# Down weights of each expert loaded from ACT's DMA queue, up weights still from SP's

## What is computed

```python
def expert_block(args):
    xb, e = args
    gate, up = jnp.split(xb @ w_up[e], 2, axis=-1)
    return (jax.nn.silu(gate) * up) @ w_down[e]
```

## Time and profile before

| | |
|---|---|
| median of three executions | 1182.05 us |
| profiled execution | 1187.32 us |
| its span, first to last instruction | 1185.6 us |
| TensorE clock granted, mean of the span | 0.936 |
| busy share PE / DVE / ACT / POOL | 86 / 81 / 53 / 43 % |
| SP's and ACT's queue, data moved | 270.65 MB / 0.20 MB |
| up loads, issue to landing, median | 128 x 1 MB, 7.0 us |
| down loads, issue to landing, median | 64 x 1 MB, 7.4 us |

### The profile page before, as it was taken

How to read it: one execution, slowest core, us unless ns; L and a number is a source line. 1 busy time by engine, 2 the same in 40 slices (tenths; PEclk the granted TensorE clock), 3 DMA queues, 4 the chain that set the end, 5 groups by cost and what they waited for, 6 DMA issues and landing times.

```text
span 1185.6 us, 15716 instructions
## 1 busy us (share of the span) xinstructions
PE 1018.2 (86%) x5224; PEld 843.9 (71%) x5224; DVE 954.8 (81%) x1003; ACT 627.0 (53%) x580; POOL 508.8 (43%) x314
## 2 busy tenths in 40 slices
PE   0888899999989985853999999999999999999960
PEld 0667679778867964853788887787877778888750
DVE  6686973995697398775788988889889899988868
ACT  1343452445345344052666776766767677776740
POOL 1343544545454454411534444664346545536110
PEclk9888999999998997855999999999999999999995
DMA  9233524432442345053889999999999999999973
GB/s 359 74 82 96 143 59 130 131 96 81 142 142 71 124 125 177 1 180 118 320 299 338 363 360 353 359 368 350 344 358 358 364 357 373 372 365 365 336 254 146
DMA packets 102892, 279.61 MB, mean 236 GB/s; under 512 B 10035, under 2 KB 59339, under 8 KB 85455
## 3 DMA queue, kind: packets, MB, share of 16 engines
q1 hardware_dynamic: 96874, 270.65, 63.9%
q0 software_dynamic: 4640, 8.41, 2.0%
q10 hardware_dynamic: 1350, 0.20, 0.1%
HBM read 275.03 MB, written 12.58 MB: 243 GB/s over the span
## 4 chain that ended last, share of the span: by engine, by line
DVE 22%; DMA 20%; PE 14%; issue 7%; ACT 6%; SPq 0%; DVEq 0%; ACTq 0%; POOLq 0%; POOL 0%
DMA moe<-in_moe_w_up 10%; DMA moe<-in_moe_w_down 9%; DVE moe_r L1105 8%; ACT moe_r L739 5%; PE ps L1546 3%; PE ps L1548 3%; PE ps L1550 2%; PE ps L1479 1%; DVE ssd L891 1%; PE ps L1504 1%; PE ps L1481 1%; PE ps L1480 1%; DVE moe L1202 1%; DVE moe_r L1208 1%; DVE moe_r L1196 1%
## 5 line engine op out<-in xcount | busy, mean ns | idle before, releaser
L1105 DVE TENSOR_TENSOR moe_r<-moe,moe_r 128x2048 fp32r<-128x2048 f32 x192 | 444.2, 2327 | 68.1 <-ACT moe_r L739 66.9
L739 ACT ACTIVATE moe_r<-moe 128x2048 fp32r<-128x2048 f32 x192 | 367.7, 1921 | 173.2 <-DMA moe<-in_moe_w_up 98.6
L1546 PE MATMUL ps<-moe_r 128*128 128x512 f32 x768 | 224.7, 401 | 8.8 <-DVE moe_r L1105 5.2
L1548 PE MATMUL ps<-moe_r 128*128 128x512 f32 x768 | 218.1, 392 | 0.0
L1550 PE MATMUL ps<-moe_r 128*128 128x512 f32 x768 | 216.6, 390 | 0.0
L449 POOL TENSOR_TENSOR ssd_r<-ssd,ssd_r 128x1024 fp32r<-128x1024 f32 x56 | 138.0, 2464 | 151.5 <-ACT ssd_r L586 151.2
L1546 PEld LDWEIGHTS ps<-moe_r 128*128 128x128 f32 x768 | 140.0, 189 | 42.8 <-DVE moe_r L1105 13.2
L1548 PEld LDWEIGHTS ps<-moe_r 128*128 128x128 f32 x768 | 145.3, 189 | 31.4
L1550 PEld LDWEIGHTS ps<-moe_r 128*128 128x128 f32 x768 | 144.8, 189 | 31.2
L1334 PE MATMUL ps<-ssd_r 128*128 128x512 f32 x320 | 132.5, 414 | 13.9 <-DVE ssd L864 13.0
L543 POOL DMA_INDIRECT ydram<-moe,moe_i x16 | 31.0, 1939 | 264.1 <-DVE moe L1214 264.1
(11 more groups left out here) (255 smaller groups left out, 1447.1 us busy)
## 6 DMA issues: line engine op xcount, KB each, us to landing
moe<-in_moe_w_up SPq DMA_DIRECT2D x128, 1024.0 KB, 7.0
moe<-in_moe_w_down SPq DMA_DIRECT2D x64, 1024.0 KB, 7.4
ssd<-in_ssd_w_in SPq DMA_DIRECT2D x40, 512.0 KB, 4.0
ssd<-in_ada_w SPq DMA_DIRECT2D x32, 512.0 KB, 3.7
ssd<-in_ssd_w_out SPq DMA_DIRECT2D x16, 512.0 KB, 3.5
ssd<-in_ada_w SPq DMA_DIRECT2D x4, 1024.0 KB, 10.0
early<-in_ada_w SPq DMA_DIRECT2D x4, 1024.0 KB, 11.8
moe<-ydram SPq DMA_DIRECT2D x8, 512.0 KB, 4.6
```

Source lines behind the costliest of these rows:

```text
L739: act.activation(wr[:, i % RING, 0, :], ring[:, i % RING, :], ACT.Identity).then_inc(s_wh, 1)
L1105: dve.tensor_tensor(wr[:, i % RING, 1, :], ring[:, i % RING, :], wr[:, i % RING, 0, :].bitcast(F32), ALU.subtract).then_inc(s_wl, 1)
L1546: mm(to[i], xh, wh[i], start=start, stop=False)
L1548: mm(to[i], xh, wl[i], start=False, stop=False)
```

## The change

The four down loads inside the loop move from SP's program to ACT's, with their waits. In each block ACT issues down 0 after copy 5, down 1 after `hidden_high`, down 2 after copy 7 and down 3 after copy 8. SP keeps the up loads, the loads of block 0 and the downs of the last block.

```diff
@@ SP, the loop
                 up_e = sp.snap(b % E)
-                dn_e = sp.snap((b + (E - 1)) % E)
                 for i in range(MU):
-                    sp.wait_ge(s_wl, moe_unit(b, i) - RING + 1)
                     if i < DC:
+                        sp.wait_ge(s_wl, moe_unit(b, i) - RING + 1)
                         load_up(up_e, i)
-                    else:
-                        load_down(dn_e, i - DC)
@@ ACT
+            def load_down(b, e, j):
+                act.wait_ge(s_wl, moe_unit(b, DC + j) - RING + 1)
+                act.dma_start(ring[:, j % RING, :].rearrange("p (k n) -> p k n", k=2),
+                              dn_v[ds(e, 1), :, 2 * j:2 * j + 2, :].rearrange("a p k n -> p (a k) n")).then_inc(ld_w[j % RING], 16)
+
             def moe(b, first, last):
+                if not first:
+                    dn_e = act.snap((b + (E - 1)) % E)
                 for i in range(3, 6):
                     high(b, i, first)
                 if not first:
+                    load_down(b, dn_e, 0)
                     hidden_high(b - 1, 0, hT)
                     hidden_high(b - 1, 1, hT)
+                    load_down(b, dn_e, 1)
                 high(b, 6, first)
                 high(b, 7, first)
                 if not first:
-                    for i in range(DC, MU - 1):
-                        high(b, i)
+                    load_down(b, dn_e, 2)
+                    high(b, DC)
+                    load_down(b, dn_e, 3)
+                    high(b, DC + 1)
+                    high(b, DC + 2)
```

More of the change, by code:

```diff
@@ L766, in gates @@
                     act.activation(sgate[:, j * 512:(j + 1) * 512], bank(j), ACT.Silu).then_inc(s_gate, 1)
+            dn_v = w_down.rearrange("l e (k p) n -> (l e) p k n", p=P)
+            def load_down(b, e, j):
+                act.wait_ge(s_wl, moe_unit(b, DC + j) - RING + 1)
+                act.dma_start(ring[:, j % RING, :].rearrange("p (k n) -> p k n", k=2),
+                              dn_v[ds(e, 1), :, 2 * j:2 * j + 2, :].rearrange("a p k n -> p (a k) n")).then_inc(ld_w[j % RING], 16)
             def moe(b, first, last):
+                if not first:
+                    dn_e = act.snap((b + (E - 1)) % E)
                 for i in range(3, 6):
```

## The result

The changed kernel takes 1191.38 us (median of 9 executions, 1186.52 to 1195.11) against 1183.24 us (1179.48 to 1186.74) for the kernel before on the same chip: a ratio of 1.0068, with a 95% interval of 1.0049 to 1.0087, so 8.1 us slower. In a second set of executions it was 1.0047 (1.0022 to 1.0071), or 5.6 us. The forecast was 4.8 us slower, "same" by a margin of 1 us; the time is inside the forecast's range (1179 to 1194), and the change is a small loss that can be measured.

A forecast was written before the change was run, and what follows sets the result against it. It took a ring slot's round trip, with PE, DVE and DMA all near full, as the bound. 0 + 0 + 2.8 + 2.0 = 4.8 us on 1182.05 gave 1186.9; forecast range 1179 to 1194, overall range 1172 to 1206.

The forecast's parts named there:

- The bound: Expert loop: PE, DVE and DMA all near full; a ring slot's round trip of about 12 us gives 36 us per block.
- Part 1: SP's queue: it loses 4 issues of 0.376 us per block, 1.5 us on a queue that mostly waits; gain 0.
- Part 2: Four issues on ACT at 0.45 us, 1.8 us per block against 9 us of idle time; charged 0 by themselves.
- Part 3: ACT's new waits: the one for low 5 delays copy 6, so low 6 starts 1.4 us later; charged 2.8 us.
- 2 short blocks: Blocks of the shortest periods, with no queue to hide in: the 1.4 us charged in full, 2.8 us together.
- just in time: Third down, leaving 1.4 us late at 828.6, was to land at 833.7 to 834.1; consumed at 834.19 before the change.
- 2.3 us of queueing: Part of a down's usual 7.4 us round; a load issued later by less than that can still land on time.
- rival 1: The wait for low 5 takes the chain in ordinary blocks too, 13 to 21 us: 1195 to 1203; chance 0.20.
- margin of 0.1 to 0.5 us: What was left between the late third down's landing and its use, in the block at 818 us.
- Part 4: Two queues at once: up 7 and the fourth down land late, low 11 starts 0.15 us late; charged 2.0 us.
- Rival 2: Queue turns favour ups; fourth down and up 7 come 2 us late for DVE and PE: 30 us, 1212; chance 0.12.
- Rival 3: Second queue keeps DMA engines moving across seams, period falls to PE's floor: 19 us faster, 1163; chance 0.14.

The follow-up runs named there:

- spread issues: The kernel before, one queue, with copy 11 moved ahead of rows_high and low 11 ahead of rows_low; ratio 0.9993.
- the kernel without the stall: The changed kernel with down 1 issued after copy 6 instead of before it, all four downs on ACT's queue; ratio 0.9985, run once more 1.0009.
- waits alone: The kernel before, all loads on SP's queue, with the change's four waits put into ACT's program and no DMA there; ratio 1.0034.

## Why the prediction was right, and where it was off

**The bound.** Three engines and the DMA engines all close to full, and a round trip of the ring as the chain: nothing in the runs speaks against it. The spread issues moved nothing, and DVE's 1.4 us per block cost something but not all.

**Part 1, SP.** Nothing was expected from it, and the kernel without the stall shows nothing (0.9985, 1.0009).

**Part 2, the issues.** Taken at 0.45 us each and as hidden. The row of after has 0.379 us for one (60 of them), and the kernel without the stall issues all four in ACT's program at no cost. The one in the stall is not hidden: it is the larger part of the difference between an idle time of 0.86 us (waits alone) and 1.41.

```profile
L769 ACTq DMA_DIRECT2D moe<-in_moe_w_down x60: 379/379/422, 600.0 to 1123.8; - x60
```

**Part 3, the stall.** The size was right: 1.4 us before low 6, measured 1.41 in every profile of the change. The term that was mis-sized is what follows. I charged it in full in the 2 short blocks and at 0 in the 13 others, 2.8 us, since low 9 would start no later and the third down would be "just in time". It costs 5.6 to 8.1 us, the whole loss. Lows 7 and 9 do give back 0.5 and 0.3 us (0.73 to 0.22, 0.47 to 0.15), but low 10 waits more (0.48 to 0.73, and 0.93 in the second set), and PE's wait for the last low part of the block, low 11, grows from 4.3 us over all blocks to 8.6 and 11.5 (from the timeline). In the kernels without the stall it is 4.7 and 3.3. Timed from the end of low 5, in us and in the mean of the 15 blocks, the path of the third down shows how it gets there:

| | before | changed | changed, second set | no stall, both runs |
|---|---|---|---|---|
| low 6 starts | 1.17 | 2.61 | 2.61 | 1.14, 1.17 |
| low 9 starts | 10.31 | 10.77 | 10.55 | 10.32, 10.32 |
| third down issued | 3.87 | 5.15 | 5.18 | 4.00, 3.95 |
| its last packet ends | 10.50 | 11.37 | 11.33 | 10.67, 10.61 |
| copy 10 starts | 11.14 | 11.84 | 11.78 | 11.28, 11.18 |
| low 11 starts | 17.67 | 18.32 | 18.32 | 17.77, 17.65 |

At low 9 most of the 1.4 us is indeed swallowed, as I had it. The step that failed is the third down. By my 2.3 us of queueing a load issued up to that much later could still land on time; issued 1.3 us later, it landed 0.8 to 0.9 later, and 0.65 us are left at low 11, or 10 us over 15 blocks. So the stall did reach the third down and its copy in ordinary blocks, by a part of its size: this is rival 1, at 0.3 to 0.6 of the 13 to 21 us that I gave it. The margin of 0.1 to 0.5 us that I worked out for that step was smaller than the spread of the rounds (5 to 11 us), and I charged nothing for the times when it isn't met.

**Part 4, the seams.** 2.0 us were charged for them. That is 0.17% of the time, less than the ratios of the kernels without the stall can tell (0.9962 to 1.0008 and 0.9991 to 1.0028), but the traces show nothing of them. The fourth down was to land 2 us late and low 11 to start 0.15 us late; its round by the packets grew by 0.2 us without the stall and by 0.3 to 0.4 with it, and DVE is idle for 0.00 to 0.02 us before low 11 (before 0.04). Up 7 was to land 1.8 us late; its round, 6.7 us before by the packets, is 6.8 to 7.5 in these four profiles. I had down 0 begin to move 1.4 us after its issue. Its first packet starts 2.1 to 2.4 us after it (2.0 before) and 1.6 to 2.2 us ahead of the end of up 7, where it was 1.9 before: the two overlap hardly more than in one queue. Rival 2's mechanism exists, but elsewhere: not where one queue hands over to the other, but where a single load lies in the second queue among its neighbours. The Trainium skill, DMA: Bandwidth & Descriptors, section "Queues, rings and completion order", has each DMA engine take turns between queues. Down 0's 9.1 and 9.2 us there agree with it, and so does the overlap of its packets with down 1's. Rival 3, a gain from the second queue, has no run for it.

**The sum.** 4.8 us were 2.8 of stall and 2.0 of seams, where the runs show 5.6 to 8.1 of stall and none of seams that they could tell. That the sum came near is in part luck: one term was too small, one too large. The median of the downs' round was to fall below 7 us. For downs 0 and 1 the medians rose from 7.7 and 8.3 us to 8.7 and 8.6, and by the packets that of all 60 went from 6.9 to 7.2, and to 6.9 in the second set. That it is unchanged or longer while the period grows is the sign that I had put down for rival 1.

## What to carry to other kernels

When an engine takes over DMA issues, price the waits before the issues: in an in-order queue a wait for the youngest result of the next engine holds up that engine's own food. Placed one copy later, where the wait is already met, the same issue had no cost here that could be measured. A walk through one block that ends "just in time" by less than the spread of the transfer times should be charged as late in part of the blocks. And where loads are needed in order, one load moved to a second queue by itself can delay its neighbours: here one of four cost 0.3 to 0.5%, and all four nothing measurable.

## What the runs showed of the hardware

Moving 60 loads of 1 MB to the second queue left the DMA engines' busy share at 0.96 and their rate at 359 GB/s (359 before), by the window of the loop in the kernel without the stall:

```profile
640.00:1120.00 480.00, 468.61 (x2164) 382.13 (x2164) 428.94 (x275) 338.21 (x236) 235.26 (x143) 1.00 0.96 359
```

The Trainium skill, DMA: Bandwidth & Descriptors, section "Issuing engines are not separate DMA queues", says that DMAs started from several engines run on the same 16 DMA engines; the equal rate agrees with it. What I had not expected is that one lone load in a second queue makes an older load of the first land 1.4 to 1.5 us later (9.1 and 9.2 us against 7.7). With all four downs in the second queue, down 0 takes only 0.2 to 0.7 us longer by the packets.
